# Query products on rows without the norm's factor in a hybrid decoder layer's mix stage

## The reference

```python
def rms_norm(x, g):
    y = xf * lax.rsqrt(jnp.mean(xf * xf, axis=-1, keepdims=True) + RMS_EPS)
    return y * g
...
mixed = concatenate([rms_norm(ssm_y, g_out_ssm), rms_norm(attn_o, g_out_attn)]) @ w_out
h = x + mixed
h = h + peer_ffn(rms_norm(h, g_ffn), peer_w_q, subkeys, peer_u, peer_v)
...
def peer_ffn(x, w_q, ...):
    q = (x @ w_q).reshape(n, 8, 2, 128)      # 2048 query columns per token
    s = einsum('nhsd,hskd->nhsk', q, subkeys) # then top-k, expert rows, gelu, weighted sum
```

## Time and profile before

| what | value |
| --- | --- |
| median of 3 runs | 2368.66 us (2366.96 to 2369.31) |
| span of the profiled execution | 2369.2 us |
| PE busy, PEld busy | 2171.8 us (92%), 1902.8 us (80%) |
| DVE busy, ACT busy, POOL busy | 1612.4, 840.5, 733.9 us |
| instructions | 36619 |

### The profile page before, as it was taken

The page is one execution under the profiler, slowest core; times in us unless marked ns, Lnnn a source line. Parts: engine busy times, 40 slices in busy tenths (PEclk is TensorE's granted clock), DMA queues, the critical chain, the costliest instruction groups (busy, mean ns, idle before and its releaser), DMA issues. The chain is left out here.

```text
span 2369.2 us, 36619 instructions
## 1 busy us (share of the span) xinstructions
PE 2171.8 (92%) x11589; PEld 1902.8 (80%) x11589; DVE 1612.4 (68%) x3723; ACT 840.5 (35%) x1573; POOL 733.9 (31%) x651
## 2 busy tenths in 40 slices
PE   7986998776789999996999899999999999999989
PEld 5555887543689999996888798888899999999978
DVE  6657122656430178998889787777898989898853
ACT  2130122552322233344887333332332323233231
POOL 0520221203123355452444222222433333333303
PEclk9997799778889999998999899999999999999999
DMA  5216433505312244444666777778888878787711
GB/s 213 25 32 146 129 116 120 163 10 169 103 63 72 89 154 137 137 136 166 196 188 200 268 300 300 296 301 329 294 297 289 301 279 304 282 307 280 269 65 41
DMA packets 194281, 448.24 MB, mean 189 GB/s; under 512 B 26433, under 2 KB 109634, under 8 KB 184642
## 3 DMA queue, kind: packets, MB, share of 16 engines
q1 hardware_dynamic: 137314, 222.02, 28.5%
q0 software_dynamic: 44288, 156.92, 19.2%
q10 hardware_dynamic: 12576, 67.97, 7.4%
HBM read 394.07 MB, written 54.80 MB: 189 GB/s over the span
## 5 line engine op out<-in xcount | busy, mean ns | idle before, releaser
L2750 PE MATMUL e_ps<-w_hi,v_hi 128*128 128x448 f32 x512 | 190.7, 372 | 11.9 <-DVE w_lo L2618 7.1
L1646 PE MATMUL e_ps<-x_hi,u_hi 128*128 128x448 f32 x512 | 187.9, 367 | 5.6 <-DVE u_lo L2548 5.6
L2439 ACT ACTIVATE v_hi<-v_raw 128x512 fp32r<-128x512 f32 x256 | 158.4, 624 | 96.3 <-PE e_ps L2762 46.4
L2762 PE MATMUL e_ps<-w_hi,v_hi 128*128 128x448 f32 x512 | 187.7, 367 | 4.1 <-issue 4.1
L2750 PE MATMUL e_ps<-w_lo,v_hi 128*128 128x448 f32 x512 | 189.1, 369 | 0.0
L2750 PE MATMUL e_ps<-w_hi,v_lo 128*128 128x448 f32 x512 | 189.1, 369 | 0.0
L1646 PE MATMUL e_ps<-x_lo,u_hi 128*128 128x448 f32 x512 | 187.7, 367 | 0.0
L1646 PE MATMUL e_ps<-x_hi,u_lo 128*128 128x448 f32 x512 | 187.7, 367 | 0.0
L2762 PE MATMUL e_ps<-w_lo,v_hi 128*128 128x448 f32 x512 | 187.5, 366 | 0.0
L2762 PE MATMUL e_ps<-w_hi,v_lo 128*128 128x448 f32 x512 | 187.4, 366 | 0.0
L1956 POOL TENSOR_TENSOR r_u_lo<-r_u_raw,r_u_hi 128x1024 fp32r<-128x1024 f32 x50 | 134.0, 2681 | 143.4 <-ACT r_u_hi L1908 143.4
(11 more groups left out here) (559 smaller groups left out, 5626.0 us busy)
## 6 DMA issues: line engine op xcount, KB each, us to landing
v_raw<-in_v_tab ACTq DMA_DIRECT2D x62, 1024.0 KB, 7.4
u_raw<-in_u_tab SPq DMA_DIRECT2D x64, 512.0 KB, 5.5
mixT<-gate_scr SPq DMA_DIRECT2D x32, 896.0 KB, 5.9
gate_scr<-gate_stage SPq DMA_DIRECT2D x13, 2048.0 KB, 9.3
r_u_raw<-in_u_tab SPq DMA_DIRECT2D x50, 512.0 KB, 3.8
gelu_scr<-mixT SPq DMA_DIRECT2D x32, 448.0 KB, 2.7
acts_and_rows<-gelu_scr SPq DMA_DIRECT2D x16, 896.0 KB, 8.2
m_w_raw<-in_w_mix SPq DMA_DIRECT2D x24, 512.0 KB, 3.5
```

The costliest lines, as they stand in the source:

```text
L1646: mm = pe.matmul(out, as_r(u), as_r(x[:, i, 0:TD]), start=(i == 0 and n == 0), stop=(i == KD - 1 and n == 2))
L2439: nc.scalar.activation(as_r(v_hi[:, c % 4]), v_raw[:, c // 4, c % 4], ACT.Copy).then_inc(v_hi_made, 1)
L2750: mm = nc.tensor.matmul(ps[:, c, 0:TD], as_r(v[:, c % 4, e]), as_r(w[b][:, e]), start=(first and e == 0 and n == 0), stop=(last and e == E ...
L2762: mm = nc.tensor.matmul(ps[:, 4 + c % 4, 0:TD], as_r(v[:, c % 4, e]), as_r(w[b][:, e]), start=(e == 0 and n == 0), stop=(e == EG - 1 and n ...
```

## The change

The query products no longer take normalised rows. Per output tile n of the first eight, DVE multiplies the new `hT` tile by the gain `g_ffn` alone (`gh`), ACT makes its high part into `gh_hi`, DVE its low part into `gh_lo`: two new buffers of eight tiles each. ACT's squares go into two turns of `sq`, and DVE adds them up into one tile `total` (`add_squares`). Tile 8 starts from `gh_hi` and `gh_lo`; behind its 48 matmuls PE sums `total` over the partitions (two matmuls with the ones), then goes on with tile 9. DVE makes mean and reciprocal, ACT the root, and DVE multiplies each query tile by `rinv` on the way from PSUM to `k.qp` (before, ACT copied it). In the same turns, 8 to 15, DVE makes the normalised rows `hn` two at a time, and the last 128 tokens of them once more into `tail`; ACT and DVE make `x_hi` and `x_lo` from `hn`. The turning of the last 128 tokens into rows moves from behind tile 9 to behind tile 17, its copy from turn 10 to turn 18. ACT's list keeps `w_high(n + 2)` at the head of each query turn, behind the wait for `ms_ready` and the root. `gh`, `hn` and `total` lie in `mixT`.

```diff
         w_raw, w_hi, w_lo = sb("m_w_raw", [P, 4, KD, P]), sb("m_w_hi", [P, 2, KD, P]), sb("m_w_lo", [P, 2, KD, P])
         ga, gf = sb("g_attn_sb", [P, 4]), sb("g_ffn_sb", [P, KD])
         rinv = sb("m_rinv", [P, T])
-        sq = sb("m_sq", [P, KD, T])
-        hn = sq
+        gh_hi, gh_lo = sb("m_gh_hi", [P, KD, T]), sb("m_gh_lo", [P, KD, T])
+        sq = sb("m_sq", [P, 4, T])
+        free = k.mixT[:].rearrange("p i t -> p (i t)")
+        gh, hn = (free[:, 2 * T * n:2 * T * n + 2 * T].rearrange("p (b t) -> p b t", b=2) for n in range(2))
+        tail = k.x_first.rearrange("p (c n) -> p c n", c=KD)
+        total = free[:, 6 * TD + D + P:6 * TD + D + P + T]
         ps = ctx.enter_context(nc.psum_tensor("m_ps", [P, 8, 512], F32))
         tile = lambda n: ps[:, 2 * (n % 3):2 * (n % 3) + 2]
...
             def x_high(c, src):
-                nc.scalar.activation(as_r(k.x_hi[:, c]), src[:, c], ACT.Copy).then_inc(x_hi_made, 1)
+                nc.scalar.activation(as_r(k.x_hi[:, c]), src, ACT.Copy).then_inc(x_hi_made, 1)
             for c in range(4):
                 nc.scalar.activation(sq[:, c], k.mixT[:, 4 + c], ACT.Square).then_inc(squared, 1)
             for c in range(4):
-                x_high(c, k.mixT)
+                x_high(c, k.mixT[:, c])
             w_high(0)
             w_high(1)
             act.wait_ge(ms_ready, 1)
             nc.scalar.activation(rinv[:], rinv[:], ACT.Sqrt).then_inc(root_ready, 1)
             for c in range(4):
                 act.wait_ge(attn_ready, c + 1)
-                x_high(4 + c, k.mixT)
+                x_high(4 + c, k.mixT[:, 4 + c])
             for n in range(OUT):
                 w_high(n + 2)
-                act.wait_ge(h_ready, n + 1)
-                nc.scalar.activation(sq[:, n], k.hT[:, n], ACT.Square).then_inc(squared, 1)
+                act.wait_ge(gh_made, n + 1)
+                nc.scalar.activation(as_r(gh_hi[:, n]), gh[:, n % 2], ACT.Copy).then_inc(gh_hi_made, 1)
+                if n >= 2:
+                    act.wait_ge(added, n - 1)
+                if n < 4:
+                    act.wait_ge(summed, 1)
+                nc.scalar.activation(sq[:, n % 2], k.hT[:, n], ACT.Square).then_inc(squared, 1)
             act.wait_ge(ms_ready, 2)
             nc.scalar.activation(rinv[:], rinv[:], ACT.Sqrt).then_inc(root_ready, 1)
-            for c in range(KD):
-                act.wait_ge(hn_ready, c + 1)
-                x_high(c, hn)
             for n in range(OUT, ALL):
                 w_high(n + 2)
-                act.wait_ge(multiplied, n + 1)
-                if n == OUT + 2:
+                c = n - OUT
+                if c < KD:
+                    act.wait_ge(hn_ready, c + 1)
+                    x_high(c, hn[:, c % 2])
+                if n == OUT + 10:
                     act.wait_ge(rows_done, 1)
-                    nc.scalar.activation(k.x_first.rearrange("p (b n) -> p b n", b=2), ps[:, 6:8, :], ACT.Copy)
-                nc.scalar.activation(k.qp[:, n - OUT].rearrange("p (h n) -> p h n", h=2), tile(n)[:, :, 0:HALF], ACT.Copy).then_inc(q_copied, 1)
+                    nc.scalar.activation(k.x_first.rearrange("p (b n) -> p b n", b=2), ps[:, 6:8, :], ACT.Copy).then_inc(rows_copied, 1)
...
             def x_low(c, src, n):
                 dve.wait_ge(x_hi_made, n + 1)
-                V.tensor_tensor(as_r(k.x_lo[:, c]), src[:, c], k.x_hi[:, c], ALU.subtract).then_inc(x_lo_made, 1)
+                V.tensor_tensor(as_r(k.x_lo[:, c]), src, k.x_hi[:, c], ALU.subtract).then_inc(x_lo_made, 1)
+            def gh_low(n):
+                dve.wait_ge(gh_hi_made, n + 1)
+                V.tensor_tensor(as_r(gh_lo[:, n]), gh[:, n % 2], gh_hi[:, n], ALU.subtract).then_inc(gh_lo_made, 1)
+            def add_squares(n):
+                dve.wait_ge(squared, 4 + n + 1)
+                if n:
+                    dve.wait_ge(added, n)
+                    V.tensor_tensor(total, total, sq[:, n % 2], ALU.add).then_inc(added, 1)
+                else:
+                    V.tensor_copy(total, sq[:, 0]).then_inc(added, 1)
+            def normalised(c):
+                if c >= 2:
+                    dve.wait_ge(x_lo_made, KD + c - 1)
+                V.scalar_tensor_tensor(out=hn[:, c % 2], in0=k.hT[:, c], scalar=gf[:, c:c + 1], in1=rinv[:],
+                                       op0=ALU.mult, op1=ALU.mult).then_inc(hn_ready, 1)
+                V.scalar_tensor_tensor(out=tail[:, c], in0=k.hT[:, c, TD:T], scalar=gf[:, c:c + 1], in1=rinv[:, TD:T],
+                                       op0=ALU.mult, op1=ALU.mult).then_inc(tail_made, 1)
             dve.wait_ge(ld, 32)
             mean_square(512, 1)
             for c in range(4):
-                x_low(c, k.mixT, c)
+                x_low(c, k.mixT[:, c], c)
             dve.wait_ge(root_ready, 1)
             for c in range(4):
                 V.scalar_tensor_tensor(out=k.mixT[:, 4 + c], in0=k.mixT[:, 4 + c], scalar=ga[:, c:c + 1], in1=rinv[:],
                                        op0=ALU.mult, op1=ALU.mult).then_inc(attn_ready, 1)
             for c in range(4, KD):
-                x_low(c, k.mixT, c)
+                x_low(c, k.mixT[:, c], c)
             for n in range(OUT):
                 dve.wait_ge(multiplied, n + 1)
                 hs = k.hT[:, n].rearrange("p (h n) -> p h n", h=2)
                 V.tensor_tensor(hs, hs, tile(n)[:, :, 0:HALF], ALU.add).then_inc(h_ready, 1)
+                if n == 0:
+                    dve.wait_ge(x_lo_made, KD)
+                dve.wait_ge(h_ready, n + 1)
+                V.tensor_scalar(gh[:, n % 2], k.hT[:, n], gf[:, n:n + 1], None, ALU.mult).then_inc(gh_made, 1)
+                gh_low(n)
+                add_squares(n)
             mean_square(D, 2)
             dve.wait_ge(root_ready, 2)
-            for c in range(KD):
-                V.scalar_tensor_tensor(out=hn[:, c], in0=k.hT[:, c], scalar=gf[:, c:c + 1], in1=rinv[:],
-                                       op0=ALU.mult, op1=ALU.mult).then_inc(hn_ready, 1)
-                if c:
-                    x_low(c - 1, hn, KD + c - 1)
-            x_low(KD - 1, hn, 2 * KD - 1)
+            for n in range(OUT, ALL):
+                dve.wait_ge(multiplied, n + 1)
+                V.tensor_tensor(k.qp[:, n - OUT].rearrange("p (h n) -> p h n", h=2), tile(n)[:, :, 0:HALF],
+                                rinv[:].rearrange("p (h n) -> p h n", h=2), ALU.mult).then_inc(q_scaled, 1)
+                c = n - OUT
+                if c < KD:
+                    normalised(c)
+                if 1 <= c <= KD:
+                    x_low(c - 1, hn[:, (c - 1) % 2], KD + c - 1)
         @block.tensor
         def _(pe):
-            def column_sums(n, first):
-                for c in range(n):
-                    pe.wait_ge(squared, first + c + 1)
-                    for h in range(2):
-                        mm = nc.tensor.matmul(ps[:, 6 + h, 0:HALF], k.ones[:], sq[:, c, HALF * h:HALF * h + HALF],
-                                              start=(c == 0), stop=(c == n - 1))
-                mm.then_inc(summed, 1)
-            column_sums(4, 0)
+            pe.wait_ge(squared, 1)
+            for c in range(4):
+                pe.wait_ge(squared, c + 1)
+                for h in range(2):
+                    mm = nc.tensor.matmul(ps[:, 6 + h, 0:HALF], k.ones[:], sq[:, c, HALF * h:HALF * h + HALF],
+                                          start=(c == 0), stop=(c == 3))
+            mm.then_inc(summed, 1)
             for n in range(ALL):
-                if n == OUT:
-                    column_sums(KD, 4)
                 pe.wait_ge(w_lo_made, n + 1)
                 if n >= 3:
                     if n - 3 < OUT:
                         pe.wait_ge(h_ready, n - 2)
                     else:
-                        pe.wait_ge(q_copied, n - 2 - OUT)
-                operands = k.x_hi, k.x_lo, w_hi[:, n % 2], w_lo[:, n % 2], tile(n)
-                if n in (0, OUT):
-                    first_products(pe, *operands, x_hi_made, x_lo_made, KD * (n // OUT)).then_inc(multiplied, 1)
+                        pe.wait_ge(q_scaled, n - 2 - OUT)
+                if n == 0:
+                    first_products(pe, k.x_hi, k.x_lo, w_hi[:, 0], w_lo[:, 0], tile(0), x_hi_made, x_lo_made, 0).then_inc(multiplied, 1)
+                elif n < OUT:
+                    up_products(pe, k.x_hi, k.x_lo, w_hi[:, n % 2], w_lo[:, n % 2], tile(n)).then_inc(multiplied, 1)
+                elif n == OUT:
+                    first_products(pe, gh_hi, gh_lo, w_hi[:, n % 2], w_lo[:, n % 2], tile(n), gh_hi_made, gh_lo_made, 0).then_inc(multiplied, 1)
+                    pe.wait_ge(added, KD)
+                    for h in range(2):
+                        mm = nc.tensor.matmul(ps[:, 6 + h, 0:HALF], k.ones[:], total[:, HALF * h:HALF * h + HALF], start=True, stop=True)
+                    mm.then_inc(summed, 1)
                 else:
-                    up_products(pe, *operands).then_inc(multiplied, 1)
```

(14 more changed lines are left out.)

## The result

The changed kernel takes 2358.03 us (median of 7 runs, 2353.98 to 2369.79), the kernel before 2369.31 (7 runs, 2366.96 to 2371.73). The ratio is 0.9956, 95% interval 0.9942 to 0.9970: faster, by 10.4 us (the interval makes it 7 to 14 us). Forecast were 16.5 us and 2352.2; the measured time lies 1.5 us above the range.

A forecast was written before the change was run, and what follows sets the result against it. PE, busy 92% of the span, was taken as the bound. Gains 21.33 - 3.05 - 1.7 - 0.1 = 16.5 us off the 2369.2 span gave 2352.7, less 0.5 for the median: 2352.2 us, range 2348.8 to 2356.5.

The forecast's parts named there:

- Steps 1 and 2: Mix stage: tile 8 starts without the norm; two sums replace 16 matmuls, 0.97 us; tile 9 starts 21.33 us earlier.
- Step 3: Ahead of tile 10: w_hi(10) stands behind the root in ACT's list, so PE waits 2.65 us for POOL's w_lo.
- Step 4: Ahead of tile 10: DVE's first hn holds up POOL's w_lo(10) by 0.4 us, making PE's wait 3.05 us.
- Step 5: Behind the wait at tile 10: PE's clock drops to about 0.6 for 3.4 us, costing 1.7 us.
- Step 6: Other mix turns: added DVE and ACT work stays hidden under 6.37 us a tile; 0.1 us later at the end.
- The sum for the stage: Mix stage: 21.33 - 3.05 - 1.7 - 0.1 = 16.5 us gained.
- so time gained here should reach the end: Mix stage: PE is the bound behind this stage too, so its gain should shorten the whole kernel.
- the stages behind it are unchanged to 1 us or so: Sign of being right: mix stage 16 to 17 us shorter, stages behind it unchanged to 1 us or so.

The follow-up runs named there:

- e4: Changed kernel with sixteen column sums on PE behind tile 8 and no adding of squares on DVE: ratio to the kernel before 0.9960, mix stage 182.7 us.
- e2: Changed kernel with ACT making w_hi of tile 10 before it waits for the mean: ratio to the kernel before 0.9920, mix stage 171.4 us.
- e5: Changed kernel with 56 more PE instructions, met waits ahead of tiles 1 to 7: ratio to the kernel before 0.9947, retrieve stage 290.0 us.
- e7: Kernel before with squares summed on DVE, two sums on PE and 56 more PE instructions: ratio to the kernel before 0.9997, retrieve stage 288.6 us.
- e8: Kernel before, its work unchanged, with 198 more PE instructions as met waits: ratio to the kernel before 1.0006, retrieve stage 289.2 us.
- e6: Changed kernel with w_hi of tile 10 ahead of the wait for the mean and 56 more PE instructions: ratio to the kernel before 0.9925.
- e9: Second profile of the changed kernel with 56 more PE instructions: span 2349.7 us, retrieve stage 288.7 us.
- e12: Third profile of the changed kernel with 56 more PE instructions: span 2349.3 us, retrieve stage 288.9 us.
- e10: Third profile of the changed kernel, unaltered, from the upper group of its runs: span 2363.5 us, experts stage 981.4 us.

## Why the prediction was right or wrong

- **Steps 1 and 2: right.** No pause between tiles 7 and 8, tile 8 in 6.4 us at 1.00. (The closest place has 692.25 - 691.1 = 1.1 us to spare by the step's own times, not 0.9; nothing hangs on it.) The two sums cost 0.75, not 0.97. e4 gives the worth of 14 sums as 6.8, 14 x 0.486.
- **Step 3: right.** Pause ahead of tile 10, ended by POOL's w_lo, behind a w_hi that starts with the root's end. e2 shows that the order in ACT's list is the cause.
- **Step 4: right in kind, too high in size.** The pause is 2.79 for 3.05: w_lo(10) took 2.70 for 2.40, so hn cost it 0.3 of the 0.4 allowed. The exclusive use that the Trainium skill describes ("SBUF — State Buffer", section "SBUF: two separate sides") is what these traces show: the tail copy took 2.44 for 0.34 behind a POOL operation, and of two that start within 0.03 us of each other one takes its usual time and the other that and 2.1 to 2.3 more.
- **Step 5: right.** 3.4 us at 0.60.
- **Step 6: right.** 6.37 us a tile in both halves; w_lo took at most 2.70. The step's chain of 5.2 leaves out ACT's gh_hi, 0.67, which stands in it; it was hidden all the same.
- **The sum for the stage: right.** 16.5 forecast, 16.7 measured in three profiles.
- **Wrong: "so time gained here should reach the end" and "the stages behind it are unchanged to 1 us or so".** PE is the bound behind the stage, and yet the retrieve stage is 4.2 us longer in each of three profiles. The step that failed is the one that put what the change does behind the mix stage at nothing: I counted the 14 sums as time only. They were 56 instructions as well, and without them a transfer of instructions falls on the first load of weights of the retrieve stage. e5, e7 and e8 show this in both directions: PE's pause is 1.39 us shorter without the transfer (4.49 to 3.10), 0.97 shorter (4.18 to 3.21), and 1.07 longer with it (3.14 to 4.21). That the load is late because it shares the DMA engines with the transfer is inferred from this and from the sizes. In the changed kernel two more things come on top: a longer half clock (6.8 for 3.4 us; in the tile itself 812.58 - 804.80 = 7.78 for 6.74, so 1.0 measured) and the extra pause from POOL and DVE (1.3 us, with what follows it 1.5). Together 1.35 + 1.04 + 1.5, of 4.2; the rest lies at the stage's end. That these two follow from the transfer isn't shown. The longer half clock was seen in four of the six profiles with it and in none of the eight without. The extra pause is decided by hundredths of a us and comes without the late load too (e5, e6).
- The range was too narrow for the same reason: no case of mine had a price for the stages behind, though I named them as what nothing prices. 16.7 - 4.2 = 12.5 from the prediction's own start would have been 2356.2, just within it; from the median of the seven runs of before, 2369.3, it is 2356.8. The rest, to the measured 2358.0, is within the spread of the runs: in nine further runs the median was 2356.3. That this spread lies in the experts stage is seen in one profile of a long run only.

## What to carry to other kernels

An edit that takes instructions off an engine moves the transfers of its instructions in time for everything behind it. Where a stage begins with a load that all engines wait for, look in the DMA view whether an instruction transfer falls on it, and count a few us either way into the range of any change ahead of it. In an engine's list, look for what stands behind a newly moved wait and needn't: here one w_hi, moved ahead of the wait for the norm, was worth 4.5 us. And compare profiles stage by stage, with more than one profile of a kernel: the runs of this kernel spread over 16 us, and the one long run that was profiled had its excess in another stage, while the mix stage of 176 us repeated to 0.1. The retrieve stage of one kernel (e5, e9, e12) had 288.7, 288.9 and 290.0, so a difference of a us there needs a second profile.

## What the runs showed of the hardware

- Behind a pause of PE the granted clock was at half for 3.4 or for 6.8 us: 3.4 us behind 2.79 to 3.50 and behind 4.21 and 4.65 us of pause, 6.8 behind 4.18, 4.36, 4.49 and 4.76. From 4.18 on both occur: 6.8 where the clock had fallen 0.7 us or more before PE resumed, 3.4 where it fell at most 0.4 before.
- A load of 512 KB, issued with three others behind it, landed for ACT 3.4 to 3.8 us after the first score product without an instruction transfer of 16 KB beside it (eight profiles), and 4.5 to 5.0 us with one (six), which itself took 0.95 to 1.43 us.
- PE's rate in the last 550 us of the experts stage was 248 matmuls in 50 us in thirteen profiles and 243 in one, e10, at full granted clock in both.
- A POOL operation of 2.40 us and a DVE operation of 2.29 with two inputs in SBUF that start within 0.03 us of each other don't share the time: one keeps its own, the other takes 4.54.
